# A two-layer transformer kernel in which three rows of normalising factors reach all partitions by GpSimd's transfers through device memory instead of by TensorE

## What is computed

```python
def rmsnorm(x, g):
    y = x * rsqrt(mean(x * x, axis=-1, keepdims=True) + EPS)
    return y * g
# first block
x = x + hybrid_mixer(rmsnorm(x, norm_mix), ...)                       # A_INPUT
x = x + memory_cross_attention(rmsnorm(x, norm_xa), rmsnorm(mem, norm_mem), ...)  # A_CROSS, A_MEMORY
x = x + squared_relu_mlp(rmsnorm(x, norm_ffn), w1, w2)                # A_FFN
x = rmsnorm(x, norm_final)
# second block
x = x + conv_and_window_attention(rmsnorm_2(x, norm_mix_w), ...)      # A_SECOND
up, gate = split(rmsnorm_2(x, norm_ffn_w) @ w_ffn_up, 2)              # A_FFN2
x = x + (silu(causal_dwconv_2(up, ...)) * gate) @ w_ffn_down
return rmsnorm_2(x, norm_final_w)
```

## Time and profile before

| | |
|---|---|
| time, median of 3 runs | 1547.36 us (1547.09 to 1548.5) |
| span of the profiled execution, first to last instruction | 1544.6 us |
| TensorE matmul busy | 1534.5 us (99%) |
| VectorE / ScalarE / GpSimd busy | 875.9 / 605.9 / 103.5 us |
| DMA mean | 95 GB/s |

### The profile page before, as it was taken

How to read it: one execution, slowest core, us unless ns; L and a number is a source line. 1 busy time by engine, 2 the same in 40 slices (tenths; PEclk the granted TensorE clock), 3 DMA queues, 4 the chain that set the end, 5 groups by cost and what they waited for, 6 DMA issues and landing times.

```text
span 1544.6 us, 20434 instructions
## 1 busy us (share of the span) xinstructions
PE 1534.5 (99%) x8150; PEld 1270.0 (82%) x8150; DVE 875.9 (57%) x1336; ACT 605.9 (39%) x979; POOL 103.5 (7%) x87
## 2 busy tenths in 40 slices
PE   9999999999999999999999999999999999999998
PEld 7888889887788888888888887877888888888887
DVE  7777766654454343436556777543555653664565
ACT  6546334533343241323556343533244331332333
POOL 0000202110020000000140000100011000000000
PEclk9999999999999999999999999999999999999999
DMA  7121213521133223222322232222332232222212
GB/s 269 56 69 35 77 69 125 189 82 57 57 106 109 94 86 107 95 97 89 108 96 68 84 114 91 94 77 69 116 104 87 99 107 96 92 99 98 93 63 74
DMA packets 44861, 146.70 MB, mean 95 GB/s; under 512 B 4960, under 2 KB 8288, under 8 KB 44640
## 3 DMA queue, kind: packets, MB, share of 16 engines
q1 hardware_dynamic: 42592, 141.93, 27.3%
q10 hardware_dynamic: 2176, 3.47, 0.7%
HBM read 143.29 MB, written 2.10 MB: 94 GB/s over the span
## 4 chain that ended last, share of the span: by engine, by line
PE 98%; issue 1%; DVE 0%; DMA 0%; ACT 0%; POOLq 0%; POOL 0%; DVEq 0%; SPq 0%; ACTq 0%
PE bank L1239 29%; PE bank L1241 29%; PE bank L1240 29%; PE bank L1457 1%; PE bank L1474 1%; PE bank L1368 1%; PE bank L1396 1%; PE bank L1401 1%; PE bank L1491 0%; PE bank L1207 0%; PE bank L1209 0%; PE bank L1208 0%; PE bank L1514 0%; PE bank L1503 0%; PE bank L1169 0%
## 5 line engine op out<-in xcount | busy, mean ns | idle before, releaser
L1239 PE MATMUL bank<-a_hi,w_hi 128*128 128x512 f32 (+1 forms) x1275 | 497.2, 390 | 0.0
L1241 PE MATMUL bank<-a_hi,w_lo 128*128 128x512 f32 (+1 forms) x1275 | 490.0, 384 | 0.0
L1240 PE MATMUL bank<-a_lo,w_hi 128*128 128x512 f32 (+1 forms) x1275 | 489.6, 384 | 0.0
L1818 DVE TENSOR_TENSOR w_lo<-w_raw,w_hi 128x1024 fp32r<-128x1024 f32 (+2 forms) x259 | 327.3, 1268 | 146.6 <-ACT w_hi L1535 146.2
L1535 ACT ACTIVATE w_hi<-w_raw 128x1024 fp32r<-128x1024 f32 (+2 forms) x259 | 266.2, 1034 | 206.8 <-PE bank L1241 198.2
L1239 PEld LDWEIGHTS bank<-a_hi,w_hi 128*128 128x128 f32 x1275 | 239.6, 188 | 49.3 <-issue 2.4
L1241 PEld LDWEIGHTS bank<-a_hi,w_lo 128*128 128x128 f32 x1275 | 239.5, 188 | 48.0
L1240 PEld LDWEIGHTS bank<-a_lo,w_hi 128*128 128x128 f32 x1275 | 239.7, 188 | 45.8 <-issue 0.2
L1239 PE MATMUL bank<-b_hi,w_hi 128*128 128x512 f32 (+1 forms) x720 | 276.5, 384 | 0.0
L1240 PE MATMUL bank<-b_lo,w_hi 128*128 128x512 f32 (+1 forms) x720 | 275.1, 382 | 0.0
L1241 PE MATMUL bank<-b_hi,w_lo 128*128 128x512 f32 (+1 forms) x720 | 275.1, 382 | 0.0
(11 more groups left out here) (319 smaller groups left out, 1198.3 us busy)
## 6 DMA issues: line engine op xcount, KB each, us to landing
w_raw<-weights_in SPq DMA_DIRECT2D x247, 512.0 KB, 3.2
w_raw<-weights_in SPq DMA_DIRECT2D x8, 384.0 KB, 2.9
x_first<-x_in SPq DMA_DIRECT2D x8, 256.0 KB, 5.9
xs<-x_in ACTq DMA_DIRECT2D x2, 1024.0 KB, 10.8
w_raw<-weights_in SPq DMA_DIRECT2D x8, 256.0 KB, 2.7
mem_x<-mem_in SPq DMA_DIRECT2D x1, 1024.0 KB, 7.8
out<-xs SPq DMA_DIRECT2D x8, 128.0 KB, 1.8
w_raw<-front_in SPq DMA_DIRECT2D x5, 192.0 KB, 5.9
```

The costliest lines, as they stand in the source:

```text
L1239: pe.matmul(to, weights_hi[:, at], hi, start=k == k0, stop=False)
L1240: pe.matmul(to, weights_hi[:, at], lo, start=False, stop=False)
L1241: t = pe.matmul(to, weights_lo[:, at], hi, start=False, stop=k == k1 - 1)
L1818: dve.tensor_tensor(lo[:, 0:size], raw[:, n % SLOTS, 0:size], hi[:, 0:size].bitcast(F32), ALU.subtract).then_inc(split_dve.handle, 1)
```

## The change

Before A_CROSS, A_FFN and A_FFN2 the step "row" has neither TensorE's four transposes nor ScalarE's copy. GpSimd, right behind its power, writes the 128x4 roots to a row of 512 numbers in device memory (`rows_between`), waits until that has landed, and reads the row back into all 128 partitions of `rstd`. The readers wait for the second transfer (`sent_row`) in place of ScalarE's copy. The step no longer takes a side bank.

```diff
+SENT_ROWS = (A_CROSS, A_FFN, A_FFN2)
...
+    if kind == "row" and n in SENT_ROWS:
+        return []
...
+        def row_ready(g):
+            return sent_row.at(2 * SENT_ROWS.index(g) + 2) if g in SENT_ROWS else row_act.at(g, 1)
...
-                elif kind == "row":
+                elif kind == "row" and n not in SENT_ROWS:
...
-                elif kind == "row" and n not in HALF_OF:
+                elif kind == "row" and n not in HALF_OF and n not in SENT_ROWS:
...
-                    q.wait_ge(*row_act.at(g, 1))
+                    q.wait_ge(*row_ready(g))
...
+                elif kind == "row" and n in SENT_ROWS:
+                    i = SENT_ROWS.index(n)
+                    q.wait_ge(*root_pool.at(n))
+                    pool.dma_start(rows_between[i].rearrange("(c p) -> p c", p=P), root_of(n)[:, 0:NC], allow_slow_non_contiguous=True
+                                   ).then_inc(sent_row.handle, 16)
+                    q.wait_ge(*sent_row.at(2 * i + 1))
+                    q.wait_ge(*rstd_used(n))
+                    pool.dma_start(rstd[:, :], rows_between[i].partition_broadcast(P)).then_inc(sent_row.handle, 16)
...
+    rows_between = nc.dram_tensor("rows_between", (len(SENT_ROWS), S), F32, kind="Internal").ap()
```

More of the change, by code:

```diff
@@ L744, in build_program @@
 def build_program(nc, x_in, mem_in, front_in, logits_in, weights_in, ws_in, columns_in, rows_in, sinks_in, matrices_in,
-                  positions_in, out):
+                  positions_in, rows_between, out):
     with ExitStack() as base:
@@ L918, in build_program @@
         root_pool = signal("root_pool", "root", lambda n: 2 if n == A_TWICE else 1)
-        row_pe = signal("row_pe", "row", lambda n: 2 if n == A_SECOND else 1)
-        row_act = signal("row_act", "row", lambda n: 2 if n == A_SECOND else int(n not in HALF_OF))
+        row_pe = signal("row_pe", "row", lambda n: 2 if n == A_SECOND else int(n not in SENT_ROWS))
+        row_act = signal("row_act", "row", lambda n: 2 if n == A_SECOND else int(n not in (*HALF_OF, *SENT_ROWS)))
+        sent_row = landing("sent_row")
         conv_dve, conv_act, taps_dve = signal("conv_dve", "conv", 2), signal("conv_act", "conv"), signal("taps_dve", "taps", TAPS1 - 1)
@@ L2153, in vector_program @@
                     q.wait_ge(*multiplied("ffn_w1", n))
-                    q.wait_ge(*row_act.at(A_FFN))
+                    q.wait_ge(*row_ready(A_FFN))
                     dve.scalar_tensor_tensor(temp("relu", n), full("ffn_w1", n), 0.0, rstd[:, :], ALU.max, ALU.mult).then_inc(relu_dve.handle, 1)
@@ L2458 @@
     out = nc.dram_tensor("out", (KT, P, S), F32, kind="ExternalOutput").ap()
-    build_program(nc, *args, out)
+    rows_between = nc.dram_tensor("rows_between", (len(SENT_ROWS), S), F32, kind="Internal").ap()
+    build_program(nc, *args, rows_between, out)
     result = run_bass_kernel_spmd(nc, [arrays], core_ids=[0]).results[0]["out"]
```

## The result

The changed kernel takes 1561.28 us in the median of four runs (1559.16 to 1561.45), against 1547.33 for the kernel before on the same chip: ratio 1.0088, 95% interval 1.0077 to 1.0100, 13.9 us slower. The direction was forecast; the size, +4.2, was not, and 1561.28 lies 1.3 above the range.

A forecast was written before the change was run, and what follows sets the result against it. TensorE's program was taken to bound the kernel; stalls of 3.55, 0.7 and 1.3 at three deadlines, less 1.3 of removed transposes, gave +4.2: 1547.36 + 4.2 = 1551.6 us. The range was 1546.0 to 1560.

The forecast's parts named there:

- What bounds the kernel: Whole kernel: TensorE is busy 99% of the span, so the time is the length of its program.
- What is taken out, 1.3: At three places: TensorE loses four transposes, 0.44 us a row, 1.3 us in all; ScalarE's copies are worth nothing by themselves.
- The first transfer, 4.5 with bounds 1.8 and 7.2: GpSimd's 512 pieces of 4 bytes to device memory: 1.8 if pieces cost nothing, 7.2 if all goes by pieces, middle 4.5.
- GpSimd's part, 0.9 + 1.3 + 0.3 on top: After GpSimd's power: 0.9 for changing kind of instruction, 1.3 for two dearer issues, 0.3 for three hand-overs.
- The second transfer, 3.0: Reading the row of 512 numbers back to 128 partitions, priced like the positions' load: 3.0 us, slowest of that form 6.8.
- C: Time from the end of GpSimd's power to the second transfer's landing in rstd: forecast 10.0 us, counted up to 13.
- Deadline 1: Memory attention, first scores needing VectorE's readings: up to 6.45 us from power to rstd is hidden; TensorE stands 3.55.
- Deadline 2: First feed-forward block, VectorE's late tiles and last b_lo: up to 9.3 us from power to rstd is hidden; TensorE stands 0.7.
- Deadline 3: Second feed-forward block, pairs and last b_lo: up to 8.7 us from power to rstd is hidden; TensorE stands 1.3.
- a sign of being wrong: In the changed kernel's trace: a wait of TensorE on w_lo would show that a deadline lies elsewhere.
- the rival I gave one chance in ten: Attention: TensorE's clock falls in the stall, 16 scores matmuls take up to 3.6 more, +7.8, 1555.2 us; chance 0.10.
- the formula: Whole kernel: change is (C - 6.45) + (C - 9.3) + (C - 8.7) - 1.3, each bracket only where positive.

The follow-up runs named there:

- the three kernels with a short first transfer: The change with 4-byte pieces 64 bytes apart by GpSimd (1545.73 us), with 16-byte pieces by GpSimd (1546.29), and with 16-byte pieces by ScalarE's queue (1546.15).
- the spacing test: The changed kernel with each 4-byte piece written 64 bytes from the next and a constant row read into rstd: 1545.73 us, 0.9995 of the kernel before.

## Why the prediction was off, point by point

**What bounds the kernel: right.** With no wait on the path the time is TensorE's program; off the path nothing moved it (16 added transfers on GpSimd, 12 on SyncE: 1546.79).

**What is taken out, 1.3: about right, 1.1 where it can be read.** The times can't tell: the three kernels with a short first transfer lie 0.4 to 0.9 below the kernel before, within their intervals. By the milestones each of the three gains 0.44 to 0.48 in each feed-forward block, where 0.44 was forecast. At the attention the one in which TensorE does not wait for `xa_q` (16-byte pieces, ScalarE's queue) gains 0.2, so 1.1 in all; why not 0.44 there stays open.

**The first transfer, 4.5 with bounds 1.8 and 7.2: this is the step that failed.** It measured 9.9, 6.9 and 8.3, above the upper bound in two places. I had scaled an ordinary store's landing by the number of pieces, because each has to be described and written. The number was wrong as a scale: 512 pieces 64 bytes apart land in 2.6 to 2.7, close to the 2.3 to 2.8 of 128 pieces of 16 bytes. What costs is that 4-byte pieces from different partitions are neighbours in device memory, and the cost is paid after the engines' last packet: 7 us of the 9.9 at the attention. That these writes are merged one after another into the same stretch of memory is my reading of the spacing test; no row shows the memory itself. The Trainium skill, "DMA: Bandwidth & Descriptors", section "Specifications", says that below 512 bytes the engines read, modify and write; by that all three forms would suffer, and the runs separate them by a factor of about three. The same page of the Trainium skill, section "Anatomy of one DMA — SWDGE (gpsimd) path", with its 2.0 us fixed plus bytes, gives an estimate of 2.0 for the first (measured 6.9 to 9.9 side by side, 2.6 to 2.7 spread out) and of 2.6 for the second (3.4 to 4.8).

**GpSimd's part, 0.9 + 1.3 + 0.3 on top: too dear.** The power's end to the issue is 0.3, and from the landing to the second issue 0.25; the issues of 0.95 and 0.57 lie inside the landings. The 0.9 rested on a wrong reading: a power's 1.01 or 1.92 does not go by the kind of instruction before it. In the trace of the kernel before

```profile
232.42 1.96 POOL L2319 TENSOR_TENSOR memory_d<-memory_s,small 128x512 f32<-128x512 f32 x1 [21.50 <-DVE memory_s L2051]
238.49 1.01 POOL L2281 TENSOR_TENSOR narrow<-narrow,columns 128x4 f32<-128x4 f32 x1 [4.12 <-DVE narrow L2063]
...
249.72 1.93 POOL L2281 TENSOR_TENSOR narrow<-narrow,columns 128x4 f32<-128x4 f32 x1 [6.05 <-DVE narrow L2063]
257.13 1.92 POOL L2281 TENSOR_TENSOR narrow<-narrow,columns 128x4 f32<-128x4 f32 x1 [5.48 <-DVE narrow L2063]
```

a power behind a multiplication took 1.01, and one directly behind another power took 1.92. What does decide stays open. The second transfer, 3.0, was 3.4 to 4.8. Together the three errors make C 13.9, 12.3 and 12.7 in place of 10.0; at the attention +5.4 for the first transfer, +0.4 for the second and -1.9 for GpSimd's part.

**Deadline 1, C = 6.45: right.** 13.9 - 6.45 = 7.45 against a wait of 7.3; moving it by a product moved the wait as it should.

**Deadline 2, C = 9.3: mis-sized by 1.5.** At C = 12.3 it gives 3.0, less 0.44: 2.6; the block lost 1.2, with two waits: 0.4 for the low part of a weight tile and 0.6 for the last `b_lo`. In the changed kernel relu 6 and relu 7 of VectorE are

```profile
494.94 0.68 DVE L2164 SCALAR_TENSOR_TENSOR temp<-bank,rstd 128x512 f32<-128x512 f32 x1
...
497.60 0.68 DVE L2164 SCALAR_TENSOR_TENSOR temp<-bank,rstd 128x512 f32<-128x512 f32 x1
```

2.66 apart and not 4.14: the last tile has no low part of a weight tile ahead of it, and I had counted five equal steps. The deadline is at 10.8; 12.3 - 10.8 - 0.44 = 1.1.

**Deadline 3, C = 8.7: right in size.** 12.7 - 8.7 - 0.44 = 3.6, measured 3.5. That the number fits is partly luck: more than half of it was paid earlier, at products waiting 0.2 for the first pair's reading and 1.2 for low parts of weight tiles, which I had said I did not expect to be late next and had named as a sign of being wrong. At the forecast C, 2.7 us shorter, these waits would not have come; that is an estimate from their lengths, and no run shows it.

**The clock: the rival I gave one chance in ten happened.** I priced it at up to 3.6 and it cost 3.0. I gave it little because at C = 10.0 the stall was to be 3.55; the clock fell in every stall of 5.7 to 7.3 that a profile shows, and no run has one near 3.5.

By the formula with the measured C's: 7.45 + 3.0 + 4.0 - 1.3 = 13.2, plus 3.0 of clock 16.2; with deadline 2 mended 14.7, against 15.0 of the span. So the deadlines were read well in the main and a price was not. Two steps put the time where it is. The first transfer moved it from +4.2 to about +12. The clock moved it past the range: the measured C's are 13.0 in the mean, just the range's upper end, and with deadline 2 mended they give 11.7 without the clock, 1559.1. The upper end of 1560 was built for a stall of 6.5 at the attention and left out what the clock costs behind it; and by its own sum, 1547.36 + 13.2, it should have been 1560.6.

## What to carry to other kernels

A detour around a busy engine is worth what it takes off that engine (here 1.3 us) and costs every deadline that it misses: find the first reader that the bounding engine waits for, and count from there, including the clock that falls when that engine stands (1.9 to 3.0 us here). A rival that the far end of a range makes likely belongs in the range. Transposing a small tensor through device memory in 4-byte pieces side by side was slow here whatever issued it (6.9 to 10.9 us); lay it out on chip so that each partition's pieces are neighbours (16 bytes were enough here), or keep the pieces apart (64 bytes here). And when no row shows an operation, a store of another shape is no upper bound for it.

## What was unexpected of the hardware

- 512 writes of 4 bytes, 2 KB in all: 6.9 to 10.9 us side by side, 2.2 to 3.8 with 64 bytes from one to the next (6.1 once), from GpSimd's, ScalarE's and SyncE's queues alike (the spread form was run on GpSimd's and SyncE's). The last packet of the 9.9 at the attention was over 7 us before the landing; in the two spread transfers whose packets were looked up the landing followed the last packet within 1.2 us.
- A transfer by GpSimd, issue to landing, is no slower than by ScalarE's queue here: 2.8, 2.3, 2.4 against 3.4, 2.4, 2.5 for the 16-byte form. Its issue is longer, 0.55 to 0.95 against 0.33 to 0.38.
